# A mixture of experts: rows scattered to memory, or added on the chip by products with a slot-to-token matrix

## What is computed

```python
weight = g_w * e_w / sum(e_w)                       # two experts a token
expert, token = ...                                 # 1024 pairs, sorted by expert
hid = silu(ragged_dot(xs, w_gate)) * ragged_dot(xs, w_up)
ys = ragged_dot(hid, w_down) * weight[order]
out = segment_sum(ys, tok_sorted, num_segments=512)
```

## Time and profile before

| what | value |
|---|---|
| runs | 2705.91, 2701.52, 2702.6 us; median 2702.6 us |
| profiled execution | span 2704.4 us from first to last instruction; no other time of it is given |
| mean granted TensorE clock | 0.975 of full |
| busy | PE 93%, weight loads 68%, DVE 40%, ACT 28%, POOL 7% of the span |
| DMA | 576.56 MB, mean 213 GB/s |
| first experts stage | first product 228.47 us, last down product starts at 703.77 us |
| second experts stage | 999.75 us, 1477.02 us |

### The profile page before, as it was taken

The page is one execution under the profiler, slowest core; times in us unless marked ns, Lnnn a source line. Parts: engine busy times, 40 slices in busy tenths (PEclk is TensorE's granted clock), DMA queues, the critical chain, the costliest instruction groups (busy, mean ns, idle before and its releaser), DMA issues.

```text
span 2704.4 us, 36859 instructions
## 1 busy us (share of the span) xinstructions
PE 2507.2 (93%) x14582; PEld 1852.0 (68%) x14582; DVE 1077.4 (40%) x1628; ACT 754.9 (28%) x1221; POOL 182.2 (7%) x302
## 2 busy tenths in 40 slices
PE   8997999788899979998788899999999999999999
PEld 7675665444576656664454677888888877888887
DVE  4753110100345641110001666656642666556542
ACT  3530000000245410000001353543332454434331
POOL 0001111111000001111111000000000010000000
PEclk9998999999999989999999999999999999999999
DMA  6339999999722189999998422222332312223231
GB/s 172 85 145 382 405 406 409 411 408 406 267 94 79 40 329 405 405 405 411 408 407 334 170 67 90 79 94 94 100 134 93 102 48 95 85 92 103 94 125 55
DMA packets 175401, 576.56 MB, mean 213 GB/s; under 512 B 20560, under 2 KB 104080, under 8 KB 125618
## 3 DMA queue, kind: packets, MB, share of 16 engines
q1 hardware_dynamic: 164722, 558.07, 54.5%
q0 software_dynamic: 10560, 16.81, 1.9%
HBM read 569.56 MB, written 23.07 MB: 219 GB/s over the span
## 4 chain that ended last, share of the span: by engine, by line
PE 68%; SPq 20%; DMA 5%; DVE 3%; issue 3%; ACT 2%; DVEq 0%; POOLq 0%; POOL 0%; ACTq 0%
PE ps L232 16%; PE ps L234 16%; PE ps L233 16%; SPq L1175 13%; SPq L1181 7%; PE ps L1325 6%; PE ps L1343 4%; DMA r_x<-resid 1%; DMA first_ring<-in_moe_w_gate 1%; PE ps L1295 1%; DMA first_weights<-in_moe_w_up 1%; ACT lat_probs L1833 1%; PE ps L1642 1%; PE ps L2330 1%; PE ps L1658 1%
## 5 line engine op out<-in xcount | busy, mean ns | idle before, releaser
L1325 PE MATMUL ps<-first_weights,moe_xsT 128*64 128x256 f32 x2688 | 311.3, 381 | 46.4 <-DMA first_weights<-in_moe_w_up 27.6
L232 PE MATMUL ps<-l_h_hi,l_w_hi 128*128 128x512 f32 x896 | 353.0, 394 | 0.0
L233 PE MATMUL ps<-l_h_lo,l_w_hi 128*128 128x512 f32 x896 | 348.8, 389 | 0.0
L234 PE MATMUL ps<-l_h_hi,l_w_lo 128*128 128x512 f32 x896 | 348.8, 389 | 0.0
L1404 DVE TENSOR_TENSOR moe_hid<-moe_silu,ps 128x256 f32<-128x256 f32 x64 | 27.0, 422 | 783.8 <-PE ps L1325 783.8
L1325 PEld LDWEIGHTS ps<-first_weights,moe_xsT 128*64 128x64 f32 x2688 | 223.9, 137 | 143.6 <-issue 93.7
L2882 DVE TENSOR_TENSOR l_w_lo<-l_raw,l_w_hi 128x2048 fp32r<-128x2048 f32 x76 | 174.1, 2293 | 270.2 <-ACT l_w_hi L2627 270.2
L1377 ACT ACTIVATE moe_ys<-ps 128x512 f32<-128x512 f32 x64 | 38.2, 597 | 678.9 <-PE ps L1343 678.9
L1343 PE MATMUL ps<-first_weights,moe_hidT 128*64 128x512 f32 x672 | 172.1, 658 | 38.3 <-DVE moe_hidT L1406 38.3
L2627 ACT ACTIVATE l_w_hi<-l_raw 128x2048 fp32r<-128x2048 f32 x76 | 145.6, 1918 | 179.4 <-PE ps L234 168.5
L232 PEld LDWEIGHTS ps<-l_h_hi,l_w_hi 128*128 128x128 f32 x896 | 168.3, 188 | 37.4 <-issue 2.9
(11 more groups left out here) (589 smaller groups left out, 4351.3 us busy)
## 6 DMA issues: line engine op xcount, KB each, us to landing
first_weights<-in_moe_w_up SPq DMA_DIRECT2D x84, 1024.0 KB
first_weights<-in_moe_w_down SPq DMA_DIRECT2D x84, 1024.0 KB
first_weights<-in_moe_w_gate SPq DMA_DIRECT2D x84, 1024.0 KB
first_ring<-in_moe_w_up SPq DMA_DIRECT2D x44, 1024.0 KB
first_ring<-in_moe_w_down SPq DMA_DIRECT2D x44, 1024.0 KB
l_raw<-in_ffn_up SPq DMA_DIRECT2D x44, 1024.0 KB, 5.1
first_ring<-in_moe_w_gate SPq DMA_DIRECT2D x40, 1024.0 KB
l_raw<-in_w_in SPq DMA_DIRECT2D x22, 1024.0 KB, 5.2
```

The costliest lines, as they stand in the source:

```text
L232: pe.matmul(out, stationary[0], moving[0], start=first, stop=False)
L233: pe.matmul(out, stationary[0], moving[1], start=False, stop=False)
L234: return pe.matmul(out, stationary[1], moving[0], start=False, stop=last)
L1325: ins = pe.matmul(k.ps[64 * h:64 * h + 64, 2 + m, 0:256], xsT[:, j, :], piece[:, j % 4, 256 * h:256 * h + 256], start=j == 0, stop=j == ND ...
```

## The change

The weights of the pairs go into the list: each is cut into three bf16 parts, the second list is a product of 250 columns instead of 100, and it now waits for them. For each slot it gives the token and the weight (`slot`). In a block, POOL copies its column of `slot` to `cur`; DVE makes `place` (128 slots by 512 tokens, 1 where the slot's token is the column); ACT makes `y_hi` = weight * y, DVE `y_lo`, the rest of it in fp32r. In the body of the next block PE multiplies `place` with both, for four tiles of 128 tokens: 16 matmuls of 64 rows x 128 x 512 fp32r, rows 0 to 63 (first half of the columns of y) and 64 to 127 (second half) in turn, into two banks. DVE adds each tile's two banks to `resid`. Scatter, read-back, diagonals and `y_dram` are gone. The last block's rows are added at the seam, tile 0 before the end of the stage. Early pieces lie in a buffer of their own, and are split in the next stage. A table of token numbers (256 KB) is loaded by ACT's queue once a stage, and DVE waits for it ahead of the first block.

```diff
@@ -321,3 +321,3 @@
             for a in range(8):
-                ins = pe.matmul(k.ps[SLOTS * h:SLOTS * h + SLOTS, 7, 0:2 * COLS], self.in_slot[:, a, :], self.in_blk[:, a, 2:4, :].rearrange("p a b -> p (a b)"),
+                ins = pe.matmul(k.ps[SLOTS * h:SLOTS * h + SLOTS, 7, 0:5 * COLS], self.in_slot[:, a, :], self.in_blk[:, a, 0:5, :].rearrange("p a b -> p (a b)"),
                                 start=a == 0, stop=a == 7)
@@ -413,5 +408,2 @@
         dve.wait_ge(x.done, 2)
-        dve.wait_ge(x.listed, 2)
-        link(dve.tensor_scalar(x.near[:, :], k.ps[:, 7, 0:COLS], k.cst[:, C_HALF:C_HALF + 1], None, ALU.add))
-        dve.tensor_tensor(r.put[:, :], x.near[:, :], k.ps[:, 7, COLS:2 * COLS], ALU.add).then_inc(x.done, 1)
         link(dve.reciprocal(x.gw[:, :], x.gs[:, :]))
@@ -419,5 +411,18 @@
         link(dve.reciprocal(x.den[:, :], x.den[:, :]))
-        link(dve.tensor_tensor(r.weight[:, 0, :], x.gw[:, :], x.den[:, :], ALU.mult))
-        link(dve.tensor_tensor(r.weight[:, 1, :], r.weight[:, 0, :], x.ratio[:, :], ALU.mult))
-        dve.wait_ge(x.done, 3)
+        link(dve.tensor_tensor(x.weight[:, 0, :], x.gw[:, :], x.den[:, :], ALU.mult))
+        link(dve.tensor_tensor(x.weight[:, 1, :], x.weight[:, 0, :], x.ratio[:, :], ALU.mult))
+        rest = x.weight[:, :, :].rearrange("p c t -> p (c t)")
+        for n in range(3):
+            link(dve.tensor_copy(x.w_part[:, n, :], rest))
+            if n < 2:
+                link(dve.tensor_tensor(x.w_rest[:, :], rest, x.w_part[:, n, :], ALU.subtract))
+                rest = x.w_rest[:, :]
+        for n in range(3):
+            ins = dve.tensor_tensor(part(2 + n), hot, over(x.w_part[:, n]), ALU.mult)
+        ins.then_inc(x.laid, 1)
+        dve.wait_ge(x.listed, 2)
+        link(dve.tensor_scalar(x.near[:, :], k.ps[:, 7, 0:COLS], float(NO_ROW), None, ALU.add))
+        dve.tensor_tensor(r.slot[:, :, 0], x.near[:, :], k.ps[:, 7, COLS:2 * COLS], ALU.add).then_inc(x.done, 1)
+        dve.tensor_reduce(r.slot[:, :, 1], k.ps[:, 7, 2 * COLS:5 * COLS].rearrange("p (n c) -> p c n", n=3), AX.X, ALU.add).then_inc(x.done, 1)
+        dve.wait_ge(x.done, 4)

@@ -553,10 +549,15 @@

-    def add(self, k, pe, t):
+    def combine(self, k, pe, t, bank, fresh):

-        pe.wait_ge(self.spread, self.norm + 1)
-        pe.wait_ge(self.y_in[t], 16 * (self.norm + 1))
-        for half in range(2):
-            for c in range(TOPK):
-                ins = pe.matmul(k.ps[:, 2 * t + half, :], self.diag[:, c, t, :], self.rows[t][:, c, half * 512:(half + 1) * 512], start=False, stop=c == TOPK - 1)
-        ins.then_inc(self.collected, 1)
+        for y in (self.y_hi, self.y_lo):
+            for h in range(2):
+                rows = slice(SLOTS * h, SLOTS * h + SLOTS)
+                ins = pe.matmul(k.ps[:, bank + h, :], self.place[rows, t * P:(t + 1) * P], y[rows, :], start=fresh and y is self.y_hi, stop=y is self.y_lo)
+        return ins
+    def add_rest(self, k, pe, t):
+        if t != 2:
+            own(k, pe, t)
+        self.combine(k, pe, t, 2 * t, False).then_inc(self.collected, 1)

@@ -1249,12 +1254,7 @@
                 weights.load(sp, layer, LAST_SET, e, free(LAST_SET, q + TURNS))
-            for m in range(2):
-                src, j = early(m)
-                sp.dma_start(k.early[:, m, :].rearrange("p (j c) -> p j c", j=j), src).then_inc(r.early_in, 16)
-            wait_then_tick(sp, ys_out, n * 16 + (EXPERTS - 1) * 16, tick_sp)
-            wait_then_tick(sp, xsT_kept, n + EXPERTS, tick_sp)
-            cl.load(sp, 0)
-            cl.load(sp, 1)
+            sp.wait_ge(used[WEIGHT_SETS - 1][5], TURNS)
+            cl.load_early(sp, 0, *early(0))
             cl.load_gains(k, sp)
-            cl.load(sp, 2)
-            cl.load(sp, 3)
+            cl.load_early(sp, 1, *early(1))

@@ -1275,2 +1275,4 @@

+                wait_then_tick(pool, ylo_made, b + 1, tick_pool)
+                pool.tensor_copy(cur[:, :, :], r.slot[:, bass.ds(b, 1), :]).then_inc(cur_set, 1)
                 wait_then_tick(pool, rows_turned, b + 2, tick_pool)
@@ -1278,9 +1280,2 @@

-                wait_then_tick(pool, ys_out, b * 16, tick_pool)
-                pool.tensor_copy(put[:, :], r.put[:, bass.ds(b, 1)]).then_inc(put_set, 1)
-                wait_then_tick(pool, put_set, b + 1, tick_pool)
-                wait_then_tick(pool, ys_kept, b + 2, tick_pool)
-                pool.indirect_dma_start(out=r.y_dram, out_offset=bass.IndirectOffsetOnAxis(ap=put[:, 0:1], axis=0),
-                                        in_=ys[:, :], in_offset=None, bounds_check=SEQ * TOPK * 2 - 1, oob_is_err=False).then_inc(ys_out, 16)
             for_each_block(pool, n, body)
@@ -1334,6 +1328,14 @@
                 for c in range(2):
-                    ins = pe.transpose(k.ps[:, 1, c * P:(c + 1) * P], hid_of_tile[:, c, :], k.ident)
+                    ins = pe.transpose(hidT_ps[:, c * P:(c + 1) * P], hid_of_tile[:, c, :], k.ident)
                 ins.then_inc(hid_turned, 1)
+                def combine(t):
+                    if not first:
+                        wait_then_tick(pe, added, b * 4 + (t - 1), tick_pe)
+                        cl.combine(k, pe, t, pair(t), True).then_inc(combined, 1)
+                wait_then_tick(pe, ylo_made, b + 1, tick_pe)
+                combine(0)
+                combine(1)
                 wait_then_tick(pe, hidT_kept, b + 1, tick_pe)
-                wait_then_tick(pe, ys_kept, b + 1, tick_pe)
                 for j in range(4):
@@ -1342,3 +1344,3 @@
                     for h in range(2):
-                        ins = pe.matmul(k.ps[64 * h:64 * h + 64, 4, :], hidT[:, j % 2, 64 * (j // 2):64 * (j // 2) + 64],
+                        ins = pe.matmul(y_ps[64 * h:64 * h + 64, :], hidT[:, j % 2, 64 * (j // 2):64 * (j // 2) + 64],
                                         weights.down[s][:, j, 512 * h:512 * h + 512], start=j == 0, stop=j == 3)
@@ -1346,2 +1348,5 @@
                         ins.then_inc(used[s][4], 1)
+                        combine(2)
+                    if j == 2:
+                        combine(3)
                 ins.then_inc(used[s][5], 1)
@@ -1355,10 +1360,10 @@
             blocks = n + (EXPERTS - 1)
-            pe.wait_ge(grown, NT)
             wait_then_tick(pe, xsT_kept, blocks + 1, tick_pe)
             wait_then_tick(pe, hidT_kept, blocks, tick_pe)
-            for t in range(2):
-                own(k, pe, t)
-            wait_then_tick(pe, ys_kept, blocks + 1, tick_pe)
+            wait_then_tick(pe, added, blocks * 4 - 3, tick_pe)
+            own(k, pe, 0)
+            wait_then_tick(pe, ylo_made, blocks + 1, tick_pe)
+            cl.combine(k, pe, 0, 0, False)
+            wait_then_tick(pe, added, blocks * 4, tick_pe)
             own(k, pe, 2)
-            own(k, pe, 3)

@@ -1373,14 +1380,8 @@
                 act.wait_ge(used[s][1], times + 1)
-                act.activation(silu[:, :], k.ps[:, 2, 0:256], ACT.Silu).then_inc(silued, 1)
-                act.wait_ge(ys_out, b * 16)
+                act.activation(silu[:, :], gate_ps, ACT.Silu).then_inc(silued, 1)
+                act.wait_ge(cur_set, b + 1)
                 act.wait_ge(used[s][5], times + 1)
-                act.activation(ys[:, :], k.ps[:, 4, :], ACT.Copy).then_inc(ys_kept, 1)
+                act.activation(cl.y_hi[:, :], y_ps, ACT.Copy, scale=slot_weight).then_inc(yhi_made, 1)

             for_each_block(act, n, body)
-            cl.diagonals(k, act)
-            act.wait_ge(r.early_in, 32)
-            for m in range(2):
-                act.activation(cl.split[m][0][:, :], k.early[:, m, :], ACT.Copy).then_inc(first_hi, 1)
-            act.wait_ge(cl.spread, cl.norm + 1)
-            act.wait_ge(first_hi, 2)

@@ -1399,16 +1401,27 @@
             dve.wait_ge(grown, NT)
+            dve.wait_ge(tokens_in, 16)

-            def body(s, times, b):
+            def body(s, times, b, first=False):
                 dve.wait_ge(silued, b + 1)
                 dve.wait_ge(used[s][3], times + 1)
-                dve.tensor_tensor(hid[:, :], silu[:, :], k.ps[:, 3, 0:256], ALU.mult).then_inc(hid_kept, 1)
+                dve.tensor_tensor(hid[:, :], silu[:, :], up_ps, ALU.mult).then_inc(hid_kept, 1)
                 dve.wait_ge(hid_turned, b + 1)
-                dve.tensor_copy(hidT[:, :, :], k.ps[:, 1, 0:256].rearrange("p (c s) -> p c s", c=2)).then_inc(hidT_kept, 1)
+                dve.tensor_copy(hidT[:, :, :], hidT_ps.rearrange("p (c s) -> p c s", c=2)).then_inc(hidT_kept, 1)
                 dve.wait_ge(rows_turned, b + 2)
                 dve.tensor_copy(xsT[:, :, :], k.ps[:, 0, :].rearrange("p (j s) -> p j s", j=ND)).then_inc(xsT_kept, 1)
+                if not first:
+                    for t in range(NT):
+                        dve.wait_ge(combined, b * 4 + (t - 3))
+                        dve.tensor_tensor(k.resid[:, t, :], k.resid[:, t, :], k.ps[:, pair(t):pair(t) + 2, :].rearrange("p b c -> p (b c)"),
```

(31 more changed lines are left out.)

130 lines of the change are left out of this document (64 added, 66 removed).

## The result

The changed kernel takes 2708.15 us in the median (2705.41 to 2709.57), the one before 2704.72 us in runs beside it (2701.52 to 2710.45). The ratio is 1.0013, with a 95% interval of 1.0007 to 1.0019: 3.4 us slower, inside the 0.2% that the prediction takes as no change. The profiled executions differ by 2.1 us (spans 2706.5 and 2704.4). I had forecast 2686.

What follows compares the result with a forecast made beforehand. Weights' DMA sets an experts stage's pace, plus two PE blocks at its end. Two stages at -1.6 us and seams at -14 give -17.2 on 2704.4; less 1.8 for the median, plus 0.6 for the table: 2686 us, range 2660 to 2714.

Steps and rivals of the forecast that it cites:

- step 3: Weights' DMA in the experts stages: cheaper scatter saves 0.42 us a block, 11.8 a stage; token table's wait hidden.
- step 6: Seams after the experts stages: statistics 5.3 us after the copy, part given back; -8 us first seam, -6 second.
- rival C: The scatter was free for the weights, pace stays 16.1 us a block: +9 us a stage, 2707; chance 0.08.
- Step 2: PE's block in the experts stages: 16 new matmuls add 1.5 us, 13.0 becomes 14.5; tiles 0 and 1 free.
- rival A: The row halves do not overlap in fp32r, PE becomes the bound: 15.9 us a block, 2763; chance 0.13.
- My two paths: Ends of an experts stage: by the weights, -2.6 us, or by PE never waiting, 699.6 against 707.5 us.
- step 5: Whole experts stage: weights' and PE's ends lie 5 us apart, 1 us added for uneven weights: -1.6 us a stage.
- rival B: Half-clock stretches in down stay, or DVE-PE waits cost as much: 14.9 us a block, 2699; chance 0.17.
- the dips: Half-clock stretches in down, 5.35 instead of 3.65 us, three in ten blocks; the forecast took none after the change.
- a first block that waits long for the table: Profile sign of a wrong forecast, which had the token table's wait at up to 2 us on PE, hidden.
- Step 1: Routing's end: second list waits for the pair weights and has 250 columns, so the weights' stream moves by +6.2 us.

Runs made afterwards that it cites:

- the three edits: Changed kernel with late table wait, run-on products in the routing's gap, tile 3's products ahead of the second seam's turn: 2681.86 us, 0.9910 of the kernel before.

## Why the prediction was wrong

The mechanism of the first seam was right, and so was that of the freed DMA time. Two steps failed. In step 3 the wait for the table was to be "hidden by the weights": it was not, and moving it gave 10.5 us in the stages. In step 6 the second seam was to give 6 us: a wait that the forecast put at nothing stood in it, and moving two calls gave 7.6. Their two gains, 18 us, are nearly the whole of the 19.3 us by which the profiled execution missed the forecast (each is shown by its own run; the two alone together were not run). The measured 2708 us is almost the number of rival C (2707), but by chance: its mechanism, a free scatter, is refuted above.

- **Step 2, PE's block, 14.5 us: measured 14.79.** The halves overlap (rival A is out) and tiles 0 and 1 are nearly free (0.16 us). The mis-sized term is tiles 2 and 3: 0.65 us each, measured 0.81 with the longer down around them, and the 0.1 to 0.2 for waits did not appear as a wait. 0.29 us a block is 9 us in 31 blocks. My two paths lay 5 us apart by step 5, so this was enough to take away the cover of everything put down as hidden. Alone it cost next to nothing: with the table's wait moved and blocks of 14.79 us the stages end 469.2 and 469.4 us after the first load, level with what the weights allow. This is the size of my rival B (14.9), without the dips: these went, as I had said.
- **Step 3, the weights.** The scatter cost 6.6 and 9.6 us a stage, counted from the first load, where I took 11.8. But the changed kernel cannot use it: it ends 475.3 and 473.8 us after the first load where its weights allow 469 to 471.
- **Step 3, the table, "up to 2 us on PE, hidden by the weights".** This is the step that failed most. The wait stopped PE for 4.11 and 1.75 us, the first block's down behind it ran at half clock for a part, and moving it won 6.1 and 4.4 us in the stages; "a first block that waits long for the table" had stood among my signs of being wrong. Its cover was the weights' path. That the cover is what counts shows in a pair of pairs: taking the wait away won 6.1 and 4.4 us with blocks of 14.79 us, and with blocks of 14.0 (high pieces only, alone and with the three edits, of which the run-on products are one more) only 1.1 and 0.1.
- **Step 1, the routing: +6.2 predicted; +6.3 to +7.1 and +4.7 to +5.0 measured.** This counts from the first product of the ranking, L307, to SP's first load: 12.7 and 13.9 us before, 19.0 to 19.8 and 18.6 to 18.8 in the changed kernel and the five edits that leave the routing as it is. The second list ends at 228.1 (I had 227.1), and the run-on products behind it took 4.27 us and not 3.4. I had charged the weights and not noticed that the run-on products, which I called unchanged, could have gone into the new gap; moving them there brings the loads 4.8 and 3.2 us forward, at a net price of about 1 us in the first block of the first stage.
- **Step 5, the stage: -1.6 predicted; +7.8 and -0.5** (the first two changes of the table above, and the fourth and fifth). It is the sum of the misses in steps 1 to 3, and in the second stage also of up to 3.5 us by which the latent layer moves by itself.
- **Step 6, first seam: -8 predicted, -8.9 measured.** Statistics at +4.8 us (I had +5.3), given back 1.05.
- **Step 6, second seam: -6 predicted, +2.7 measured.** The statistics came as foreseen, 4.8 us behind the copy. I had read what is put between them and the first product (pieces, splits), but not the new wait: ACT's squares of tile 1 for tile 3's products, which stand in PE's queue behind a turn that waits for DVE. Changing the order of two calls gave 7.6 us at the first product. Another 2.3 us are half clock behind the long idling, which I had not priced. The diff showed the wait and the order; I gave both nothing.

Together, by the table: +1.8 and +7.6 in the first stage, -0.9 at its seam, -2.0 and +3.1 in the second stage, +8.7 at the second seam, +1.0 in the rest: 19.3 us, which is 2.1 measured less -17.2 predicted. The 1.0 us of the rest is within what two executions differ: with the same code there, it took 1186.9 us in the run without slot products.

What stays open: why the kernel before had stretches at half clock in down and none of the later ones has in the middle of a stage. It is not the fill of the gap with products, as step 2 argued, since without any slot product there is none either; there PE idles 0.76 us ahead of down instead of 0.91. Whether these 0.15 us decide was not tried.

## What to carry to other kernels

Where two paths lie within a per cent of each other, a term that is "hidden" is hidden only while its cover lasts: price it also for the case that the other path wins, and add it up before calling the gain safe. Full DMA engines do not show that DMA is the bound; whether the engine that consumes ever waits for it does. And when work is moved to an engine's queue at a seam, go through every wait that the diff adds and ask what stands ahead of its producer in that queue: here two lines in the other order gave 7.6 us in the trace, and nearly 9 by the ratios (1.0013 against 0.9981).
